# Cache attention of a decoder step: VectorE's rotary sum between the two tiles' sums, and the last sequence's mean and logarithm in other pairs

## The reference

```python
def mla_keys(ckv, kpe, w_uk, g_kn):
    k_nope = jnp.einsum('btc,chd->bthd', ckv, w_uk)
    k_pe = jnp.broadcast_to(kpe[:, :, None, :], k_nope.shape[:3] + (QK_ROPE_DIM,)).astype(k_nope.dtype)
    return rms_norm(jnp.concatenate([k_nope, k_pe], axis=-1), qk_gain(g_kn))

# mla_attend_sample, for every page and then for the new token:
k = mla_keys(ckv_blk, kpe_blk, w_uk, g_kn).astype(jnp.float32)
s = jnp.einsum('bqhd,bkhd->bhqk', qf, k) * scale
m_new = jnp.maximum(m, jnp.max(s, axis=-1))
p = jnp.exp(s - m_new[..., None])
l = l * alpha + jnp.sum(p, axis=-1)
acc = acc * alpha[..., None] + jnp.einsum('bhqk,bkc->bhqc', p, ckv_blk.astype(jnp.float32))
```

## Time and profile before

| | |
|---|---|
| median of 3 runs | 2224.79 us (2221.44 to 2226.43) |
| the profiled execution's own time | 2227.32 us |
| its span | 2225.3 us |
| granted TensorE clock, mean | 0.991 |
| PE busy | 2162.5 us, 97% |
| PE's weight loads | 1804.2 us, 81% |
| DVE busy | 1528.4 us, 69% |
| ACT busy | 972.0 us, 44% |
| POOL busy | 706.6 us, 32% |

### The profile page before, as it was taken

How to read it: one execution, slowest core, us unless ns; L and a number is a source line. 1 busy time by engine, 2 the same in 40 slices (tenths; PEclk the granted TensorE clock), 3 DMA queues, 4 the chain that set the end, 5 groups by cost and what they waited for, 6 DMA issues and landing times.

```text
span 2225.3 us, 33856 instructions
## 1 busy us (share of the span) xinstructions
PE 2162.5 (97%) x12537; PEld 1804.2 (81%) x12537; DVE 1528.4 (69%) x2353; ACT 972.0 (44%) x2273; POOL 706.6 (32%) x765
## 2 busy tenths in 40 slices
PE   8999899999999999999999989999999999999999
PEld 7987566788787878787878767799999999977776
DVE  4446676688888888888888775666767767654345
ACT  4445565565565656565656553321112121133333
POOL 2554111367574747474747351100000000000000
PEclk9999999999999999999999999999999999999999
DMA  5200100242232313131314032221111111044353
GB/s 170 60 27 1 60 16 20 88 157 103 75 104 69 110 60 119 48 130 46 133 46 145 25 119 94 87 72 47 47 47 47 43 42 47 29 172 138 138 187 126
DMA packets 95811, 183.20 MB, mean 82 GB/s; under 512 B 9416, under 2 KB 65568, under 8 KB 87311
## 3 DMA queue, kind: packets, MB, share of 16 engines
q1 hardware_dynamic: 79933, 96.53, 13.5%
q0 software_dynamic: 15744, 84.93, 11.3%
HBM read 167.39 MB, written 14.36 MB: 82 GB/s over the span
## 4 chain that ended last, share of the span: by engine, by line
PE 69%; DVE 6%; issue 2%; POOL 2%; ACT 1%; DMA 0%; SPq 0%; POOLq 0%; ACTq 0%; DVEq 0%
PE ca_banks L1766 25%; PE ca_banks L2370 22%; PE ca_banks L2643 11%; PE ca_banks L1826 4%; PE ca_banks L1742 3%; PE ca_banks L1778 3%; DVE ca_cells L2219 1%; DVE ca_lo L2099 1%; POOL ca_product L1634 1%; DVE ca_cells L2214 1%; ACT ca_banks L2014 1%; PE ca_banks L2619 0%; DVE ca_w_o_lo L2129 0%; POOL ca_cells L1646 0%; DVE ca_top L2231 0%
## 5 line engine op out<-in xcount | busy, mean ns | idle before, releaser
L2014 ACT ACTIVATE ca_banks<-ca_banks 128x512 f32<-128x512 f32 x512 | 298.2, 583 | 330.4 <-PE ca_banks L1766 329.4
L1766 PE MATMUL ca_banks<-cache_w_hi,ca_hi 128*128 128x512 f32 x1024 | 428.6, 419 | 13.1 <-DVE ca_lo L2099 7.7
L2214 DVE TENSOR_REDUCE ca_cells<-ca_banks 128x8 f32<-128x512 f32 x512 | 346.2, 686 | 131.2 <-ACT ca_banks L2014 129.0
L1766 PE MATMUL ca_banks<-cache_w_lo,ca_hi 128*128 128x512 f32 x1024 | 403.8, 394 | 0.0
L1766 PE MATMUL ca_banks<-cache_w_hi,ca_lo 128*128 128x512 f32 x1024 | 402.1, 393 | 0.0
L1766 PEld LDWEIGHTS ca_banks<-cache_w_hi,ca_hi 128*128 128x128 f32 x1024 | 193.4, 189 | 55.4 <-DVE ca_lo L2099 14.8
L1766 PEld LDWEIGHTS ca_banks<-cache_w_hi,ca_lo 128*128 128x128 f32 x1024 | 193.7, 189 | 46.6
L1634 POOL TENSOR_TENSOR ca_product<-cache_kpe,attn_q_row_odd 128x512 f32<-128x512 f32 x128 | 168.4, 1320 | 180.5 <-DVE ca_cells L2219 179.5
L1766 PEld LDWEIGHTS ca_banks<-cache_w_lo,ca_hi 128*128 128x128 f32 x1024 | 194.2, 190 | 32.5
L1634 POOL TENSOR_TENSOR ca_product<-cache_kpe,ca_q_row_even 128x512 f32<-128x512 f32 x128 | 164.8, 1293 | 143.6 <-DVE ca_cells L2219 142.4
L2099 DVE TENSOR_TENSOR ca_lo<-ca_banks,ca_hi 128x512 fp32r<-128x512 f32 x256 | 174.0, 680 | 39.7 <-ACT ca_hi L1917 39.5
(11 more groups left out here) (400 smaller groups left out, 4339.3 us busy)
## 6 DMA issues: line engine op xcount, KB each, us to landing
ca_down_raw<-in_w_down SPq DMA_DIRECT2D x44, 512.0 KB, 3.4
keep_w_uv<-in_w_gate SPq DMA_DIRECT2D x22, 512.0 KB, 3.9
ca_up_raw<-in_w_up SPq DMA_DIRECT2D x22, 512.0 KB, 3.7
keep_ctx<-in_w_down SPq DMA_DIRECT2D x22, 512.0 KB, 3.7
late_room<-in_x_prompt SPq DMA_DIRECT2D x8, 512.0 KB, 3.6
ca_m<-mixed_scratch SPq DMA_DIRECT2D x8, 512.0 KB, 5.3
ca_w_raw<-in_w_o SPq DMA_DIRECT2D x16, 256.0 KB, 2.8
ca_x<-in_x_prompt SPq DMA_DIRECT2D x8, 512.0 KB
```

What stands on the lines that cost most here:

```text
L1766: last = nc.tensor.matmul(KK[:, t, :], x[:, n % 2, t, ck, :], w[:, par, ck, :], start=(m == 0), stop=(m == 5))
L2014: nc.scalar.activation(SQ[:, t, :], KK[:, t, :], ACT.Square).then_inc(squared, 1)
L2214: nc.vector.tensor_reduce(ss[:, par, 2 * n + t, :], SQ[:, t, :].rearrange("p (h d) -> p h d", d=DN), AX.X, ALU.add).then_inc(summed, 1)
```

## The change

On VectorE the two sums of a pair are parted. The first tile's sum comes directly behind `lo`; then whatever extra work the pair has (the next sequence's weights, the tail, the splits of w_o and of the mixed tile); then the rotary sum; then the second tile's sum, and every fourth pair the sum of the rotary squares. Before, the order was: the next sequence's weights, both sums, the rotary sum, the rotary squares, the tail, the splits.

In the last sequence, POOL's mean of the first 48 tiles is issued behind product 25 instead of product 26, and their norm behind product 28 instead of 29; the raw scores stay behind product 26 and the scaling behind 29. ScalarE's logarithm and exponential for them are issued in pair 28 instead of 27.

```diff
@@ POOL, sequence
+                    if b == NB - 1 and n == 25:
+                        tail_mean(b, *PARTS[0])
                     if b == NB - 1 and n == 26:
-                        tail_mean(b, *PARTS[0])
                         tail_raw(b, *PARTS[0])
+                    if b == NB - 1 and n == 28:
+                        tail_norm(b, 0, *PARTS[0])
                     if b == NB - 1 and n == 29:
-                        tail_norm(b, 0, *PARTS[0])
                         tail_scale(b, *PARTS[0])
@@ ScalarE, sequence
-                    if n == 27 and b == NB - 1:
+                    if n == 28 and b == NB - 1:
                         guess_norms(b, 0, *PARTS[0])
@@ VectorE, sequence
-                    if n == 0 and later:
-                        sums(1 - par, b - 1, PAIRS - 1)
+                    if n >= 1:
+                        sums(par, b, n - 1, (0,))
+                    elif later:
+                        sums(1 - par, b - 1, PAIRS - 1, (0,))
                     if n in FRESH_AT and b < NB - 1:
                         refresh(b + 1, FRESH_AT.index(n))
...
                         refresh_lo(b + 1, LO_AT.index(n))
-                    if n >= 1:
-                        sums(par, b, n - 1)
-                    if n >= PRODUCT_LAG:
-                        rotary_scores(par, b, n - PRODUCT_LAG)
-                    elif later:
-                        rotary_scores(1 - par, b - 1, PAIRS - PRODUCT_LAG + n)
-                    if n % 4 == 3:
-                        rotary_sums(par, b, n // 4)
                     if later:
                         tail(1 - par, b - 1, n)
                     if b == NB - 1:
...
                             split_mixed(0)
+                    if n >= PRODUCT_LAG:
+                        rotary_scores(par, b, n - PRODUCT_LAG)
+                    elif later:
+                        rotary_scores(1 - par, b - 1, PAIRS - PRODUCT_LAG + n)
+                    if n >= 1:
+                        sums(par, b, n - 1, (1,))
+                    elif later:
+                        sums(1 - par, b - 1, PAIRS - 1, (1,))
+                    if n % 4 == 3:
+                        rotary_sums(par, b, n // 4)
```

## The result

| | before | after |
|---|---|---|
| median | 2224.79 us (5 runs, 2221.41 to 2226.43) | 2210.82 us (5 runs, 2206.76 to 2214.46) |
| ratio, 95% interval | | 0.9943 (0.9929 to 0.9958) |
| the profiled execution's own time, span | 2227.32, 2225.3 | 2210.82, 2209.0 |
| granted TensorE clock, mean | 0.991 | 0.993 |

The change gained 14.0 us of the 17.6 forecast. Outside it two profiles of one and the same code differ: the keys of pair 0 start anywhere from 409.0 to 415.5 us in the profiles of this study, and the work behind the projection's start took 901 to 909.

What follows compares the result with a forecast made beforehand. TensorE was taken to bound the kernel (busy 111.99 of 112.83 us per sequence), so only its waits could yield gains: 12.5 from the rotary sum's order plus 5.1 from the last sequence, 17.6 us, giving 2207.2; range 2203 to 2214.

Steps and rivals of the forecast that it cites:

- likeliest case: Whole kernel: both the sequences and the last sequence gain, 17.6 us in all, median 2207.2; chance 0.70.
- first rival: Last sequence: VectorE's added wait on ScalarE eats the gain there, leaving only 12.5 us, 2212.3; chance 0.12.
- four stalls: Pairs 3, 10, 12 and 22: VectorE's order makes keys late by 0.43, 0.30, 0.49 and 0.55, together 1.77 us per sequence.
- I price this at nothing in sequences 0 to 6: Two-operand VectorE operations, sequences 0 to 6: no longer meeting POOL's product was counted as 0 us, the room being enough.
- refresh stall of sequence 0: Sequence 0, which has no tail: its only stall, put at 0.6 us, was to go.
- thinnest cover: Busy stretch with gathers: POOL's product 21 is done some 0.6 us before the earlier rotary sum reads it; no cost.
- That pair only falls back to the old position: Gather stretch: if POOL's product comes late, the pair merely returns to the rotary sum's old position.
- my sign of being wrong: VectorE's rotary sum waiting for POOL, or the last stretch taking 47 us or more, would show the forecast wrong.
- my slower rival: Gather stretch: half of 84 pairs held by late POOL products, 21 us lost, net 2228 to 2230; chance 0.05.
- the chain: Last sequence: splits wait for ScalarE's high half; keys two pairs on at 6.95 instead of 6.44, pairs 19 to 31 43.0 us.
- the meetings: Last sequence, iterations 26, 27, 29, 30: splits collide with POOL's mean, raw and norm, 0 to 1.09 each, 1.1 us in all.
- The clock: Last sequence: TensorE's granted clock, 0.83 behind the wait at pair 27, becomes 1.00 once that wait goes.

Runs made afterwards that it cites:

- rotary_only: The kernel before with only the rotary sum moved between the two sums, extras and splits left where they were; 2209.75 us, ratio 0.9937.
- lo_first: The kernel after with the next sequence's low weights (`refresh_lo`) directly behind `lo`, ahead of the first sum; 2208.47 us, ratio 0.9926.
- splits_late: The kernel after with the last sequence's splits behind the second tile's sum and the rotary squares; 2215.45 us, ratio 0.9953.
- pool_only: The kernel before with only the POOL and ScalarE moves of the last sequence, VectorE's order unchanged; 2217.17 us, ratio 0.9974.
- gather_early: The kernel after with POOL's gathers in sequence 0 waiting for one tile's sum less; 2209.55 us, ratio 0.9932.
- order_only: The kernel after with POOL and ScalarE as in the kernel before, so VectorE's new order alone; 2216.63 us, ratio 0.9962.

## Why the prediction was right, and where it wasn't

The time was in the range, at the upper edge of the likeliest case (2203 to 2211); the forecast was 3.5 us too low in the stage. By the median alone the first rival's 2212.3 would fit as well; it is the parts of the stage that decide between them.

- **What bounds, and the four stalls: right.** rotary_only shows the cause by itself: nothing but the rotary sum's place changed, and a sequence became 1.80 shorter, where I had read 1.77 off the four pairs. In the kernel after, these four gains are there in full; 0.37 is taken off by the new meeting, hence 1.43.
- **"I price this at nothing in sequences 0 to 6": the step that failed, 2.2 us.** I had asked only where a two-operand operation stood *behind* the rotary sum. The new place was to be free because the product starts at once; but at 718.43 `refresh_lo` stands 3.2 us behind the last rotary sum (715.21) and still meets a product, for POOL had gathers ahead of it (until 718.62). lo_first, which changes only this place, gives 0.37 per sequence back.
- **The refresh stall of sequence 0: its size right by luck, its cause and its gain wrong, 1.5 us.** I had put it at 0.6 by likeness with pair 22 of the other sequences. But keys 22 of sequence 0 came 3.22 behind the last ones in the kernel before; what it lost, 0.60, it lost at keys 24, whose rotary sum had waited 1.01 for product 21. I had named that product the thinnest cover, "done some 0.6 us before it is read", read off a middle sequence; the wait stood in the trace of before. The new order doesn't remove such a wait, and puts sum 1 behind it. "That pair only falls back to the old position" was wrong too: it fell 0.91 behind it. A rotary sum that waits for POOL was also my sign of being wrong, and the mechanism of my slower rival, met in one pair where that rival had half of 84.
- **The last sequence: the time right (5.2 against 5.1), and the chain too.** The distances of keys 19 to 31 were foretold as 4.01, 3.25, 3.70, 3.25, 4.04, 3.25, 3.71, 3.26, 4.03, 3.52, 3.45, 3.52 and came as 4.08, 3.33, 3.62, 3.36, 3.94, 3.33, 3.63, 3.36, 3.97, 3.52, 3.45, 4.49. Of the meetings, priced at 1.1 in all, one came, at 0.98. What I had not said is whose gain it is: 5.24 come from the POOL and ScalarE moves without the order, which then takes 0.85 back. The first rival (the added wait eats the gain) was thus true of a part: the wait costs, less than the old meetings before pair 25 and more than the few behind it. Its size was not 1.4 in each pair: behind a first one of 1.39, VectorE idled 0.16 to 0.51 ahead of the other eleven splits of the loop (such as the one below), for it came to them later than K+2.9. The distances came right all the same, as they hang on the time of ScalarE's high half.

```profile
1279.31 0.75 DVE L2135 SCALAR_TENSOR_TENSOR ca_w_o_lo<-ca_w_raw,keep_g_out,ca_w_o_hi 128x512 fp32r<-128x512 f32 x1 [0.50 <-ACT ca_w_o_hi L1949]
```

- **The clock: right.** Granted 1.00 where the earlier trace rows had 0.83; the wait of 3.32 us that stood in front of the slow products is gone.
- **The meetings.** A VectorE operation that meets a product ends 0.55 to 0.57 us behind the product's end: 720.50 against 719.93 (`refresh_lo`), 1273.09 against 1272.54 (splits_late), 1279.01 against 1278.46 (pool_only). The Trainium skill (SBUF — State Buffer, section SBUF: two separate sides) says of a VectorE operation with two SBUF inputs and a GpSimd operation that reads SBUF that the one that starts first has the shared pair of ports for its whole instruction, and the other "fully blocks". On the full block the traces agree. On who is first they are divided: at 1281.32 VectorE is shown 0.22 ahead and POOL paid, at 718.43 it is shown 0.21 ahead and paid itself.

The halves' gains add up to 10.09 + 5.33 = 15.4 where the whole has 14.1. The difference is in the last sequence (1.34 + 5.24 against 4.39), less 0.7 that the whole gains before the projection. It stays open what sets the outcome of two starts so close. It wasn't tried whether the 2.06 behind the projection's start have to do with the change; gather_early, whose last sequence is that of after, has 908.99 us there and after has 904.59, which speaks against it.

## What to carry to other kernels

Put an operation that releases another engine's work into a slot where its own engine idles, and look at what stands directly behind it: if that is a two-input operation in SBUF and the released work is POOL's, the two collide. When an instruction that reads another engine's work is moved ahead of others, they stand behind its wait too: look at the *first* and the least regular pass of the loop, for there a wait that the usual pass covers can be open. And split a change before giving a gain to a part: here one half earned the last stretch and the other took a piece of it back, and one edit out of the whole, the rotary sum's place, did as well as all of it.

## What the runs showed of the hardware

- A VectorE operation with two SBUF inputs that overlapped a GpSimd product took up to 1.4 us more (0.68 to 2.08, `refresh_lo` in the kernel after), and another such pair of nearly equal starts went the other way (in pool_only 1.66 instead of 1.28 for the product). Reductions with one input kept 0.66 to 0.70 in the kernel after, beside products or not.
- Behind an idle 3.3 us TensorE ran the next products at half its clock: granted 0.52 over 5.76 us in the kernel before and 0.64 over 4.77 in order_only, with products 0.43 us apart instead of 0.23 (in order_only only the first nine of the twelve), which is 1.2 GHz against 2.4. The same wait cost 1.0 us more in one profile than in the other, by how soon the clock came back. Behind the idle 2.72 us of rotary_only the clock stayed at 1.00.
